# Expert weights of a routed feed-forward kernel: slot 1 moved from SP's list to ScalarE's queue, with one load in every round

## The reference

```python
def moe_ffn(h, w_rg, b_rg, w_re, b_re, w_gate, w_up, w_down):
...
    top_v, top_i = lax.top_k(e_sel, TOP_K_IN_GROUP)
    gate = g_w * jax.nn.softmax(top_v, axis=-1)
    expert = g_idx[:, None] * EXPERTS_PER_GROUP + top_i.astype(jnp.int32)
...
    def expert_block(args):
        xblk, e = args
        hid = jax.nn.silu(xblk @ w_gate[e]) * (xblk @ w_up[e])
        return hid @ w_down[e]
```

## Time and profile before

| | before |
|---|---|
| median of three executions | 4523.62 us |
| profiled execution | 4518.43 us |
| span of the profiled execution, first to last instruction | 4516.6 us |
| TensorE, VectorE, ScalarE, GpSimd busy, share of the span | 88%, 32%, 20%, 3% |
| mean granted TensorE clock | 0.951 |
| DMA, mean over the span | 148 GB/s |
| read from HBM | 610.98 MB |

### The profile page before, as it was taken

The page is one execution under the profiler, slowest core; times in us unless marked ns, Lnnn a source line. Parts: engine busy times, 40 slices in busy tenths (PEclk is TensorE's granted clock), DMA queues, the critical chain, the costliest instruction groups (busy, mean ns, idle before and its releaser), DMA issues. The chain is left out here.

```text
span 4516.6 us, 49964 instructions
## 1 busy us (share of the span) xinstructions
PE 3965.4 (88%) x19346; PEld 1972.1 (44%) x19347; DVE 1438.1 (32%) x2683; ACT 901.2 (20%) x1892; POOL 122.3 (3%) x199
## 2 busy tenths in 40 slices
PE   5997888899998889999779798998699997888985
PEld 2564665454445554453554333332344443323333
DVE  2486666213204660431563311111221123111114
ACT  3003454102002331300451211111110012111111
POOL 0000000000000000000000000000100000000001
PEclk8998999999999999999999899998899998999997
DMA  6211222001100000110320497889800005998795
GB/s 260 109 38 40 102 103 113 28 22 38 55 38 19 1 1 28 47 47 37 133 102 2 173 383 281 310 327 412 338 19 37 37 20 213 377 414 334 281 396 201
DMA packets 79550, 668.30 MB, mean 148 GB/s; under 512 B 9504, under 2 KB 11368, under 8 KB 45216
## 3 DMA queue, kind: packets, MB, share of 16 engines
...
HBM read 610.98 MB, written 55.05 MB: 147 GB/s over the span
## 5 line engine op out<-in xcount | busy, mean ns | idle before, releaser
L258 PE MATMUL banks<-arena 128*128 128x512 f32 (+2 forms) x4544 | 1750.4, 548 | 57.5 <-ACTq L137 30.4
L258 PEld LDWEIGHTS banks<-arena 128*128 128x128 f32 x4544 | 842.6, 191 | 959.2 <-issue 889.2
L2273 PE MATMUL banks<-arena 128*64 128x512 f32 x3136 | 737.6, 628 | 138.4 <-DMA arena<-in_w_gu 136.3
L2273 PEld LDWEIGHTS banks<-arena 128*64 128x64 f32 x3136 | 233.3, 145 | 633.8 <-issue 461.6
L2290 PE MATMUL banks<-arena 128*64 128x512 f32 x1568 | 347.3, 595 | 0.0
L1511 PE MATMUL banks<-arena 128*64 128x128 f32 x1952 | 158.3, 285 | 83.9 <-DVE arena L1524 44.4
L2343 DVE COPY arena<-banks 128x256 f32<-128x256 f32 x98 | 41.1, 420 | 499.1 <-PE banks L2280 499.1
L2290 PEld LDWEIGHTS banks<-arena 128*64 128x64 f32 x1568 | 108.4, 137 | 203.9 <-issue 203.9
L937 DVE SCALAR_TENSOR_TENSOR arena<-arena 128x1024 f32<-128x1024 f32 x240 | 195.9, 878 | 0.2 <-DVEq L137 0.2
L2319 ACT ACTIVATE arena<-banks 128x256 f32<-128x256 f32 x98 | 37.6, 383 | 666.9 <-PE banks L2273 666.9
L1511 PEld LDWEIGHTS banks<-arena 128*64 128x64 f32 x1952 | 102.2, 136 | 136.7 <-ACT arena L1524 71.7
...
## 6 DMA issues: line engine op xcount, KB each, us to landing
arena<-in_w_gu SPq DMA_DIRECT2D x132, 2048.0 KB
arena<-in_w_dn SPq DMA_DIRECT2D x66, 2048.0 KB, 11.7
arena<-in_w_ada SPq DMA_DIRECT2D x24, 2048.0 KB, 7.3
y_tok<-arena ACTq DMA_DIRECT2D x196, 128.0 KB, 9.0
...
arena<-in_ab_w_ada SPq DMA_DIRECT2D x6, 2048.0 KB, 9.3
arena<-in_cd_w_ada SPq DMA_DIRECT2D x6, 2048.0 KB, 7.3
arena<-in_cd_w_in SPq DMA_DIRECT2D x6, 2048.0 KB, 7.3
```

Of the source, the lines that this page charges most:

```text
L258: last = pe.matmul(self.bank_of(g, n), lhsT, rhs, start=k == 0, stop=k == KT - 1)
L2273: last = pe.matmul(bank(2 + s_)[64 * h:64 * h + 64, :], xbT[:, k, 64 * s_:64 * s_ + 64], w_gu[s_][:, k, h], start=k == 0, stop=k == KT - 1 ...
```

## The change

Slot 0 is still loaded by a list on SP, which now holds only slot 0's entries. Slot 1 is loaded by ScalarE: its first expert at the end of `route_act`, after slot 0's half A and half B have landed, and then in each round but the last the expert of the next round, whether it is another one or not: both halves after `copy_x`, `w_dn` after the stores. The landing semaphores are split by slot, and TensorE waits for slot 1's by the number of the round. The table gets the expert of every block (`AT_EXP`) and the number of rounds less one; the expert's number is now found as an intersection of two comparisons (experts without blocks are passed over in both forms). Some semaphores of other stages are merged (`zeroed`, `pool_ld`, `ev_ld`, `passed`) and waited for at the same places. The order of the experts is that of their numbers, as before.

```diff
@@ -2032,8 +2043,9 @@
...
         place = c("place", NBLK)
-        for i, col in enumerate((exp_of, place[:, 3:4], place[:, 4:5])):
-            pe.matmul(bank(7)[0:1, LOADS * i:LOADS * i + LOADS], col, one_l, start=True, stop=True)
+        for at_, col in ((AT_E, exp_id), (AT_POS, place[:, 2:3])):
+            pe.matmul(bank(7)[0:1, at_:at_ + LOADS], col, one_l, start=True, stop=True)
+        pe.matmul(bank(7)[0:1, AT_EXP:AT_EXP + NBLK], exp_id, ident[0:NBLK, 0:NBLK], start=True, stop=True)
         pe.matmul(bank(7)[0:1, AT_RANK:AT_RANK + NBLK], rank, ident[0:NBLK, 0:NBLK], start=True,
@@ -2059,8 +2071,8 @@
...
         pe.matmul(bank(7)[:, 0:32], n_blk, c("expert_before", 32), start=True, stop=True)
-        pe.matmul(bank(7)[:, 32:64], n_blk, c("expert_upto", 32), start=True,
-                  stop=True).then_inc(m_pb, 1)
+        pe.matmul(bank(7)[:, 32:64], n_blk, c("expert_upto", 32), start=True, stop=True)
+        pe.matmul(bank(7)[:, 64:65], n_blk, ones[0:32, 0:1], start=True, stop=True).then_inc(m_pb, 1)
 
@@ -2083,6 +2095,12 @@
...
             a.dma_start(t["h_tok"][128 * i:128 * i + 128, :], h_tok[:, i % 2]).then_inc(m_tw[i % 2], 16)
+        a.wait_ge(m_tg, l + 1)
+        e = self.expert(a, 0)
+        for part, landed in ((0, self.wa), (1, self.wb)):
+            a.wait_ge(landed[0], 32)
+            self.load_gu(a, 1, e, part)
+        self.load_dn(a, 1, e)
         for tw in m_tw:
@@ -2149,19 +2167,24 @@
...
         d.wait_ge(m_pb, l + 1)
-        link(d.tensor_copy(ends, bank(7)[:, 0:64]))
+        link(d.tensor_copy(ends, bank(7)[:, 0:65]))
         first_round, side = (c("place", NBLK)[:, i:i + 1] for i in range(2))
         upto = ends[0:NBLK, 32:64]
-        link(d.tensor_scalar(cmp_b, c("iota_pair"), ends[:, 63:64], None, ALU.is_lt))
+        link(d.tensor_scalar(cmp_b, c("iota_pair"), ends[:, 64:65], None, ALU.is_lt))
         link(d.tensor_reduce(rounds_n, cmp_b, X_AXIS, ALU.add))
         link(d.tensor_scalar(blk_of, side, rounds_n[0:NBLK], first_round, ALU.mult, ALU.add))
-        for out, op in ((exp_of, ALU.is_le), (exp_bf, ALU.is_lt)):
-            link(d.tensor_scalar(cmp_b[0:NBLK], upto, blk_of, None, op))
-            link(d.tensor_reduce(out, cmp_b[0:NBLK], X_AXIS, ALU.add))
-            link(d.tensor_scalar(out, out, float(E - 1), None, ALU.min))
+        link(d.tensor_scalar(cmp_b[0:NBLK], upto, blk_of, None, ALU.is_lt))
+        link(d.tensor_reduce(exp_bf, cmp_b[0:NBLK], X_AXIS, ALU.add))
+        link(d.tensor_scalar(cmp_b[0:NBLK], upto, blk_of, None, ALU.is_le))
+        link(d.tensor_reduce(exp_of, cmp_b[0:NBLK], X_AXIS, ALU.add))
+        link(d.tensor_scalar(cmp_c, ends[0:NBLK, 0:32], blk_of, None, ALU.is_le))
+        link(d.tensor_tensor(cmp_c, cmp_c, cmp_b[0:NBLK], ALU.subtract))
+        link(d.tensor_tensor(cmp_c, cmp_c, c("iota", NBLK)[:, 0:32], ALU.mult))
+        link(d.tensor_reduce(exp_id, cmp_c, X_AXIS, ALU.add))
         link(d.tensor_tensor(fresh, exp_of, exp_bf, ALU.not_equal))
...
         link(d.tensor_tensor(fresh, fresh, valid, ALU.max))
+        link(d.tensor_tensor(fresh, fresh, side, ALU.is_gt))
         link(d.tensor_scalar(valid, first_round, rounds_n[0:NBLK], None, ALU.is_lt))
@@ -2193,7 +2216,9 @@
...
         link(d.tensor_copy(moe_tab[:, 0:AT_ROUNDS], bank(7)[0:1, 0:AT_ROUNDS]))
-        d.tensor_copy(moe_tab[:, AT_ROUNDS:AT_ROUNDS + 1], rounds_n[0:1]).then_inc(m_tg, 1)
+        d.tensor_copy(moe_tab[:, AT_ROUNDS:AT_ROUNDS + 1], rounds_n[0:1])
+        d.tensor_scalar(moe_tab[:, AT_ROUNDS + 1:AT_ROUNDS + 2], rounds_n[0:1], -1.0, None,
+                        ALU.add).then_inc(m_tg, 1)
         link(d.scalar_tensor_tensor(out=dest16, in0=bef16, scalar=float(BLK), in1=rank16, op0=ALU.mult,
@@ -2214,26 +2239,35 @@
...
         for landed in (self.wa, self.wb, self.wd):
-            sp.sem_inc(landed, 16)
-        n = sp.value_load(moe_tab[0:1, AT_RANK + NBLK - 1:AT_RANK + NBLK], min_val=2, max_val=LOADS)
+            sp.sem_inc(landed[0], 16)
+        n = sp.value_load(moe_tab[0:1, AT_RANK + NBLK - 2:AT_RANK + NBLK - 1], min_val=1, max_val=LOADS)
         with sp.Fori(0, n) as j:
             e = sp.value_load(moe_tab[0:1, bass.ds(AT_E + j, 1)], min_val=0, max_val=E - 1)
-            at_ = sp.value_load(moe_tab[0:1, bass.ds(AT_SLOT + j, 1)], min_val=YT, max_val=STAGE)
             pos = sp.value_load(moe_tab[0:1, bass.ds(AT_POS + j, 1)], min_val=0, max_val=NBLK - 1)
-            for part, landed, free in ((0, self.wa, self.free_a), (1, self.wb, self.free_b)):
+            for part, landed, free in ((0, self.wa[0], self.free_a), (1, self.wb[0], self.free_b)):
                 sp.wait_ge(landed, 16 * j + 16)
...
                 sp.sem_inc(self.passed, 1)
-                sp.dma_start(arena[:, bass.ds(at_ + UNIT * part, UNIT)],
-                             t["w_gu"][self.l, bass.ds(e, 1), :, UNIT * part:UNIT * part + UNIT].rearrange(
-                                 "e p n -> p (e n)")).then_inc(landed, 16)
-            sp.wait_ge(self.wd, 16 * j + 16)
+                self.load_gu(sp, 0, e, part)
+            sp.wait_ge(self.wd[0], 16 * j + 16)
             sp.sem_inc(self.passed, 1)
...
             sp.sem_inc(self.passed, 1)
-            sp.dma_start(arena[:, bass.ds(at_ + 2 * UNIT, UNIT)],
-                         t["w_dn"][self.l, bass.ds(e, 1)].rearrange("e p n -> p (e n)")).then_inc(self.wd, 16)
+            self.load_dn(sp, 0, e)
+
+    def load_gu(self, eng, slot, e, part):
+        eng.dma_start(mem(SLOTS[slot] + UNIT * part, UNIT),
+                      t["w_gu"][self.l, bass.ds(e, 1), :, UNIT * part:UNIT * part + UNIT].rearrange(
+                          "e p n -> p (e n)")).then_inc((self.wa, self.wb)[part][slot], 16)
+
+    def load_dn(self, eng, slot, e):
+        eng.dma_start(mem(SLOTS[slot] + 2 * UNIT, UNIT),
+                      t["w_dn"][self.l, bass.ds(e, 1)].rearrange("e p n -> p (e n)")
+                      ).then_inc(self.wd[slot], 16)
+
+    def expert(self, a, j):
+        return a.value_load(moe_tab[0:1, bass.ds(AT_EXP + 2 * j + 1, 1)], min_val=0, max_val=E - 1)
 
@@ -2261,13 +2295,13 @@
...
         with pe.Fori(0, n) as j:
-            need = [pe.value_load(moe_tab[0:1, bass.ds(AT_RANK + 2 * j + s_, 1)], min_val=1, max_val=LOADS)
-                    for s_ in range(2)]
+            rank_ = pe.value_load(moe_tab[0:1, bass.ds(AT_RANK + 2 * j, 1)], min_val=1, max_val=LOADS)
+            need = [16 * rank_ + 16, 16 * j + 16]
             pe.wait_ge(self.xe["A"], j + 1)
...
                 for part, landed, free in ((0, self.wa, self.free_a), (1, self.wb, self.free_b)):
-                    pe.wait_ge(landed, 16 * need[s_] + 16)
+                    pe.wait_ge(landed[s_], need[s_])
                     for k in range(4 * part, 4 * part + 4):
@@ -2283,7 +2317,7 @@
...
                 pe.wait_ge(self.he, 2 * j + s_ + 1)
-                pe.wait_ge(self.wd, 16 * need[s_] + 16)
+                pe.wait_ge(self.wd[s_], need[s_])
                 pe.wait_ge(self.ye[s_], j + 1)
@@ -2307,24 +2341,35 @@
...
 
+    def round_act(self, a, j, last, n):
+        e = None if last else self.expert(a, j + 1)
+        for s_ in range(2):
+            a.wait_ge(self.free_b, 2 * j + s_ + 3)
+            a.activation(sg[:, s_], bank(2 + s_)[:, 0:256], ACT.Silu).then_inc(self.sg, 1)
+        self.copy_x(a, "A", j + 1)
+        if not last:
+            for part in range(2):
+                self.load_gu(a, 1, e, part)
+        a.wait_ge(self.free_d, 2 * j + 3)
+        a.wait_ge(self.yw[0], 32 * j + 32)
+        a.activation(y_sb[:, 0], bank(6), ACT.Copy).then_inc(self.ye[0], 1)
+        a.wait_ge(self.ye[0], j + 2)
+        self.store_y(a, 0, j)
+        a.wait_ge(self.ye[1], j + 2)
+        self.store_y(a, 1, j + n)
+        if not last:
+            self.load_dn(a, 1, e)
+
     def blocks_act(self, a):
...
         n = self.rounds(a)
+        before = a.value_load(moe_tab[0:1, AT_ROUNDS + 1:AT_ROUNDS + 2], min_val=1, max_val=ROUNDS - 1)
         self.copy_x(a, "A", 0)
-        with a.Fori(0, n) as j:
-            for s_ in range(2):
-                a.wait_ge(self.free_b, 2 * j + s_ + 3)
-                a.activation(sg[:, s_], bank(2 + s_)[:, 0:256], ACT.Silu).then_inc(self.sg, 1)
-            self.copy_x(a, "A", j + 1)
-            a.wait_ge(self.free_d, 2 * j + 3)
-            a.wait_ge(self.yw[0], 32 * j + 32)
-            a.activation(y_sb[:, 0], bank(6), ACT.Copy).then_inc(self.ye[0], 1)
-            a.wait_ge(self.ye[0], j + 2)
-            self.store_y(a, 0, j)
-            a.wait_ge(self.ye[1], j + 2)
-            self.store_y(a, 1, j + n)
+        with a.Fori(0, before) as j:
+            self.round_act(a, j, False, n)
+        self.round_act(a, before, True, n)
         for s_ in range(2):
```

More of the change, by code:

```diff
@@ L43 @@
 ROUNDS = NBLK // 2
-LOADS = 40
+LOADS = E
 UNIT = KT * 512
@@ L62 @@
                   ("head_ones", 128), ("expert_before", 32), ("expert_upto", 32), ("full_blocks", S // BLK + 1),
```

(61 more changed lines are left out.)

13 lines of the change are left out of this document (6 added, 7 removed).

## The result

The kernel with the change takes 4631.6 us (median of 4 runs, 4630.07 to 4633.69), the kernel before beside it 4527.09 us (4 runs): a ratio of 1.0234, 95% interval 1.0222 to 1.0246. The forecast was 4614 us and slower. The profiled execution took 4632.01 us against 4518.43, so 113.6 us are to be found between the two traces.

A forecast was written before the change was run, and what follows sets the result against it. It took full DMA engines to bound double reloads in a row, SP's list to cost lone ones. Terms 86 - 20 + 20 + 4 = +90 us on 4518.4, plus 5.2 offset, gave 4614 us; range 4550 to 4665.

The forecast's parts named there:

- The bytes (+86, less 20): Expert rounds: 15 more slot 1 loads, 94.4 MB, cost +86.0 us over 47 rounds; idle engine time returns 20.
- the credit: Idle DMA time in light rounds (slot 1 alone reloads) takes the next round's transfers: at most 82 us, a quarter taken, -20.
- near 0.97 with 420 GB/s: Sign of being right: DMA share of the two expert stages near 0.97, at 420 GB/s.
- d1 leaves after the stores ... at nothing in light rounds: Slot 1's `w_dn`, issued about 2 us after the round's end, wanted 16 us later: no cost in light rounds.
- My price for the two kinds: Rounds where both slots reload take 31.4 us (30 of them); those reloading slot 1 alone take 22.4 us (17).
- TensorE's waits on `w_gu`: Sign of being right: these waits, on the gate and up weights, grow from 136.3 us to over 200.
- light rounds of 25 us: Sign of being wrong: rounds reloading slot 1 alone last above 25 us, with ACT waiting for `y_tok`.
- The rival built on that, 4699 us: ACT's queue: halved rate beside SP's, `yw` holds ACT, light rounds pay 5 us in 17; +175 us, chance 0.10.
- lone double reloads: Rounds where both slots change expert, the round before not; 29.9 and 30.8 us, where SP's one list costs time.
- The faster rival: SP's list was the cost: twelve lone double reloads lose about 8 us each, added loads hide; -76, 4448 us, chance 0.04.
- The starts (+20): Stage starts: route close waits for slot 0's halves, first matmul about 15 us later, some given back; 10 us, twice.
- The `w_in_odd` loads (+4): Next stage's two 2048 KB loads on SP compete with slot 1's last loads: between 0 and 9.8 us, +4.

The follow-up runs named there:

- e1: Kernel before, with every round of slot 1 counted as fresh: 81 loads, all on SP's one list; 4606.06 us, 1.0193.
- e8: Kernel after, with its repeats, slot 1's `w_dn` issued ahead of the `y_tok` stores; 4634.37 us, 1.0231.
- e5: Kernel after, slot 1 loaded only where its expert changes, first loads behind the route close, `w_dn` issued when its buffer is free, ahead of stores; 4505.28 us, 0.9953.
- e4: Kernel after, slot 1 loaded only where its expert changes, its first three loads moved behind the route stage's close; 4533.12 us, 1.0025.
- e11: Same kernel as e5, run again in five executions beside the kernel before; 4502.7 us, 0.9947.
- e3: Kernel after, slot 1's first three loads moved from the route stage to the head of the block stage; 4611.9 us, 1.0198.
- e2: Kernel after, ScalarE loading slot 1 only where its expert changes, start still in the route stage; 4557.09 us, 1.0079.

## Why the prediction was right, and where it was not

**The bytes (+86, less 20).** Right in the sum, wrong in the credit. The 47 rounds rose by 84.9 us to 1321.7; the prediction's 30 x 31.4 + 17 x 22.4 gave 1322.8 before anything was taken off. The step "I take a quarter of the credit: -20" is what failed: e1, 1321.3, has none, the kernel after has none, and e8, 1318.1, has 5 us at most. Idle time of the engines in light rounds was indeed used (DMA share 0.97 for 0.88), but what heavy rounds got of it, 31.4 to 29.9, light rounds paid. The credit of 82 us, of which a quarter was taken, was worked out at 428 GB/s throughout. The sign "near 0.97 with 420 GB/s" came only in its first half: the share is 0.97 and 0.96, the rate 403 and 398 GB/s (e1: 0.99 and 0.96, 408 and 395). At e1's share some 32 us of the 1321.3 were idle (0.01 of 680.9 and 0.04 of 640.4), not 82. Why a full share moves less over whole stages than in single heavy rounds stays open.

**Which rounds wait.** The step that failed is "d1 leaves after the stores ... at nothing in light rounds". Light rounds cost 17 x 2.6 = 44 us more than 22.4, heavy ones 30 x 1.5 = 45 less than 31.4. My price for the two kinds was met in e1 (31.3 and 22.4), where there is one queue. With two, slot 1's `w_dn` takes 20.4 us to land (median), 21.8 in the round shown, for 11.7 before. So the list of signs was wrong in two places: TensorE's waits on `w_gu` fell where I wanted over 200 us, and light rounds of 25 us, named as a sign against me, came, but not with "ACT waiting for `y_tok`". The rival built on that, 4699 us, had the right queue and the wrong victim: the stores land in 19.1 us for 9.0, and it is the load behind them that is late. Its ScalarE waiting for stores came only in e5 and e8, where `w_dn` goes first (124.6 and 145.4 us).

**The list.** Right that SP's order costs lone double reloads: e4 brings five of them from a mean of 29.5 us to 24.4, 5 us each. The faster rival was right that a queue for slot 1 helps them, and wrong twice: the added loads do not hide, and its price of 8 us each for twelve, 96 us, is too high. With the repeats out and the order on ScalarE mended, all 47 rounds together gain 18.4 us (e5), and the kernel is 0.5% faster (e11). (By the prediction's own definition there are thirteen lone ones; it shows the thirteenth, at 3136.20, among those in a row.)

**The starts (+20).** Measured +27.6 in the profiled executions; e3 puts 15 and e4 against e2 24 on it. The delay of the first matmul, 18.1 us from 2574.88 to 2593.0, or 15.8 of it counted from SP's first load, is what was worked out (15). The mis-sized term is what comes back: the first round took 25.2 us (2593.01 to 2618.19) in place of 26.6, not 22.4. TensorE was busy in all of it, but after 28.3 us of idle for 13.1 before, and at a granted clock of 0.89 where the same round had 0.93 before: its first 64 matmuls took 16.68 us, which at 7.04 for 32 would be 14.08. Of 5 us hoped for 1.4 came in the first stage and 2.4 in the second.

**The small terms.** The `w_in_odd` loads (+4): the time between the two stages did not grow (559.4 us from the last round of layer 0 to the next first load, 559.8 before), so nothing. Routing arithmetic: nothing, as said.

In sum: 84.9 + 27.6 + 1.1 = 113.6 against a forecast of 90. Of the 23.6 us missed 18.9 are the credit (84.9 for 66), 7.6 the starts (27.6 for 20) and 1.1 the rest, less the 4 of the tail. The forecast of 4614 looks closer, 17.6 us off, by luck: it added 5.2 us because the profiled execution before was that much under its median, and the profiled one after lies at its median (4632.01 and 4631.6). By medians the change is 104.5: 70 to 84 for the repeats, 15 to 24 for the start, and 10.6 for the split, which is itself a gain in lone reloads and a loss of 28 us (e4 to e5) by the order on ScalarE's queue, the later issue of `w_dn` in it.
